# Two edits of an already tuned two-block kernel: first weight halves rounded and split ahead of the mixed groups in the front, and output-projection parts spread over twelve steps of the neighbourhood attention, ahead of each value product

## The chip, the cores and the metric

The kernel runs on one core of one Trainium2 chip. The metric is device time in microseconds (us). All data are 32-bit floats. Engines in the profile: PE is the matrix engine, PEld its weight loads, DVE the vector engine, ACT the scalar engine, POOL the general engine, SP the engine that issues most DMAs.

## The reference

One call runs a block of two layers and then a second block, each on 256 tokens of width 1024. The first layer mixes with a Fourier transform, and this is the front of the kernel:

```python
def mix(h):                       # h = modulate(rms_norm(x), shift, scale)
    hg = h.reshape(b, l, FNET_GROUPS, FNET_GROUP_DIM)          # 8 groups of 128
    y = jnp.fft.fftn(hg, axes=(1, 3), norm='ortho').real
    return y.reshape(b, l, D_MODEL) @ w_out + b_out
x = x + g1 * mix(h);  x = x + g2 * swiglu(...)                 # the context tokens likewise
...                                                            # second layer: differential attention, swiglu
```

Shift, scale and gates are columns of `silu(c) @ w_ada + b_ada`. The second block projects its input once, runs a latent attention (`y_mla`, 8 heads) and a neighbourhood attention (`y_na`, 16 heads), and ends with

```python
h_res = h_res + jnp.concatenate([y_mla, y_na], axis=-1) @ w_out[l]
```

Of this last product the latent half (`y_mla`) can be formed before the neighbourhood attention is done.

## The kernel before

**How a weight gets to PE.** Each float product is made of three products of shorter floats: with `wh` the rounded weight and `wl` the rest, and `hh`, `hl` the same of the activation, `product` (L496 to L500) issues `wh*hh`, `wh*hl` and `wl*hh` into one PSUM bank. SP loads weights in slabs of 1 MB into four slots of `raw`; a slab has two halves. `round_half` (L476) lets ACT write a half into `wh`, and `split_low` (L483) lets DVE write `wl = raw - wh`. There are four slots of `wh` and `wl`, so halves 0 to 3 can stand ready at once.

**What sets the order.** Every engine runs a list written out by hand, strictly in the order of the code; engines meet at semaphores (`split` counts halves split, `s_f2v` groups split, `s_part` parts added, and so on). There is no scheduler: a moved line of code is a moved instruction on that engine, and what stands behind a waiting instruction waits too.

**The front.** x and the context are turned by PE; ACT and DVE make sums and differences of token halves; `fnet_inner(g)` (L2291) transforms group g over tokens into bank 4 or 5, and ACT (even g, L1723) or DVE (odd g, `inner_out`, L1977) copies it into `ab`. DVE scales two groups at a time by gain and shift (`inner_scaled`, L1985 to L1989). `fnet_outer(g)` (L2305, L2307) transforms over the 128 channels into bank 4 + g % 2. Then per group: ACT copies the sines and the edge columns (L1733, L1734; `s_f2q`), DVE writes `mixed` from cosines and sines (L2002, L2003; `s_f2d`), ACT rounds `mixed` to `hh` (L1739; `s_f2a`), DVE subtracts to `hl` (L2006; `s_f2v`). The last four DVE steps of a group stand in one function, `outer_split`. `fnet_dense(k)` multiplies group k by the first four halves of `fnet_w_out`: for m = 0 to 3 three products into bank m; with k = 0 each m first waits for `split` to reach m + 1. PE's list there: outer(0), outer(1), ada_slab(4), ada_slab(5), dense(0), ada_slab(6), ada_slab(7), outer(2), ada_turn(1), dense(1), outer(3), dense(2), and on to dense(7).

**The modulation weights in the front.** `ada_slab(i)` (L2245) multiplies a 1 MB slab of `w_ada`, 24 of them in the front; they pass through slots of `raw`, `big` and `ex`, and SP issues a load (L1502) only when the slab before it in its slot has been used. Weight slabs of `fnet_w_out` (L489) share SP's list: slabs 0 and 1 after ada slabs 0 and 1 are used, slabs 2 and 3 after ada slabs 6 and 7 are used.

**The neighbourhood attention.** `na_pe`, `na_act` and `na_dve` run steps i = 0 to 19; 16 of them have scores. In step i PE forms the scores of step i (L1325), turns the weights of step i - 2 (L1337, L1340; "the turn"), in even steps multiplies by the values (L1351, L1356; "the value product") and then runs `latent_part(g, k)` (L1296 to L1298) as often as `PART_AT[i]` says. A part is three products of 512 columns into bank 7; four parts (k = 0 to 3) make a quarter g of the latent output, and DVE adds it to `x_tok` (`latent_added`, L1311). Part (g, 0) waits for the quarter before it to be added (`s_part`). The value product waits for ACT's copies of the turned weights (L1384, L1386), ACT's copy in an even step waits for the value product of that step, and parts of g = 3 free the first halves of the output weights, whose successors ACT rounds in steps 13 to 16 (`ROUND_AT`).

Of the kernel before, what the change touches and what calls it, by code (L numbers as in the profile page):

```python
# [185 lines left out]
def build(nc, d, out):  # L186

    with ExitStack() as ctx:
# [1088 lines left out]
        PART_AT, parts = {}, [(g, k) for g in range(4) for k in range(4)]  # L1277
        for i in range(4, 15):
            n = 1 + i % 2
            PART_AT[i], parts = parts[:n], parts[n:]  # L1280
# [32 lines left out]
        def na_pe(pe, tail):  # L1313

            pe.wait_ge(s_gap, 1)
            for i in range(NA_STEPS + 4):
# [11 lines left out]
                if 2 <= i < NA_STEPS + 2:  # L1328
# [10 lines left out]
                    for c in range(2):  # L1339
                        ins = nc.tensor.transpose(ps[0:n, 4 + j0 % 2, (2 + c) * P:(3 + c) * P],  # L1340
                                                  ex3[:, j0 % 3, c, side:side + n], T["ident"])
                    ins.then_inc(s_tr, 1)
                if i % 2 == 0 and 0 <= (i - 4) // 2 < 8:
                    f = (i - 4) // 2
# [13 lines left out]
                    ins.then_inc(s_pv, 1)  # L1358
                for g, k in PART_AT.get(i, ()):
                    latent_part(pe, g, k)  # L1360
                tail(i)
# [321 lines left out]
        def _(act):  # L1683
# [37 lines left out]
            for g in range(0, KD, 2):  # L1721
                act.wait_ge(s_f1, g + 1)
                nc.scalar.activation(ab[:, g, :, :].rearrange("p s n -> p (s n)"), ps[:, 4, :], ACT.Copy)\  # L1723
                    .then_inc(s_f1a, 1)
            for q in range(2):
                round_half(act, q, q)
            for g in range(KD):
                act.wait_ge(s_f2, g + 1)
                if g >= 2:
                    act.wait_ge(s_f2v, g - 1)  # L1730
                m = mixed[:, g % 2, :].rearrange("p (s n) -> p s n", s=2)
                b = 4 + g % 2
                nc.scalar.activation(sines(g), ps[:, b, 2 * P + 2:4 * P], ACT.Copy)  # L1733
                nc.scalar.activation(m[:, :, 0:P + 1:P],  # L1734
                                     ps[:, b, 0:2 * P + 2].rearrange("p (s n) -> p s n", s=2)[:, :, 0:P + 1:P],
                                     ACT.Copy).then_inc(s_f2q, 1)
                act.wait_ge(s_f2q, g + 1)
                act.wait_ge(s_f2d, g + 1)
                nc.scalar.activation(by_column(hh[:, g, 0:NT]), by_row(mixed[:, g % 2, :]), ACT.Copy).then_inc(s_f2a, 1)  # L1739
                if g < AHEAD - 2:  # L1740
                    round_half(act, g + 2, g + 2)
            for m, q in enumerate(FNET_OUT_Q):
# [125 lines left out]
        def _(dve):  # L1868
# [30 lines left out]
            def ada_copy(gi):  # L1899

                dve.wait_ge(s_adau, ADA_GROUPS[gi]["end"])
                positive(dve, s_adat, gi)
                nc.vector.tensor_copy(ada_row, ps[:, 6, :]).then_inc(s_adac, 1)
# [87 lines left out]

            def outer_split(g):

# [8 lines left out]
                nc.vector.tensor_tensor(m[:, :, 1:P], cos[:, :, 1:P], sin, ALU.subtract)  # L2002
                nc.vector.tensor_tensor(m[:, :, L - 1:P:-1], cos[:, :, 1:P], sin, ALU.add).then_inc(s_f2d, 1)  # L2003
                dve.wait_ge(s_f2a, g + 1)
                dve.wait_ge(s_f2d, g + 1)
# [16 lines left out]
            inner_out(7)  # L2022
            inner_scaled(2)
            split_low(dve, 0, 0)
            outer_split(0)
            split_low(dve, 1, 1)
            outer_split(1)
            split_low(dve, 2, 2)
            split_low(dve, 3, 3)
            ada_copy(1)  # L2030
            outer_split(2)
            ada_group_out(1)
            dve.wait_ge(s_adav, 4)
            scaled_gain(0, 0, 4, 4)
            inner_scaled(4)
            outer_split(3)
            inner_scaled(6)
            for g in range(4, KD):
                outer_split(g)
            ada_copy(2)  # L2040
# [183 lines left out]
        def _(pe):  # L2224
# [71 lines left out]
            def fnet_outer(g):  # L2296
# [3 lines left out]
                if g < 2:  # L2300
                    pe.wait_ge(s_f1v if g else s_f1a, 4)
                else:
                    pe.wait_ge(s_f2v, g - 1)
                o = ps[:, 4 + g % 2, :]
# [332 lines left out]
```

## Time and profile before

| | |
|---|---|
| median of 3 runs | 1225.83 us (1225.41 to 1228.3) |
| the profiled execution, whole | 1225.37 us |
| its span, first to last instruction | 1223.7 us |
| PE busy | 1163.9 us, 95% |
| DVE, ACT, POOL busy | 716.5, 547.3, 92.9 us |
| share of PE in the chain that ended last | 82% |
| HBM | 180.48 MB read, 148 GB/s over the span |

All clock readings in the text are microseconds from the span's start in this one execution. The profiled execution lies 0.46 us under the median.

### The profile page before, as it was taken

Reading aid. Unit: us, or ns where it says so; the run is one execution under the profiler, and the core shown is the slowest. Engines: PE = TensorE matmul, PEld = TensorE weight load, DVE = VectorE, ACT = ScalarE, POOL = GpSimd, SP = SyncE. Lnnn points to the kernel's source line nnn. Section 1 sums busy time; section 2 is a strip of 40 time slices with the busy share of each in tenths; the row PEclk is TensorE's granted clock in tenths of the full one; section 3 lists DMA queues with packets and bytes.
Section 4 is the critical chain, followed back from the end, with each engine's and each line's share of the span. In section 5 each row is a group of like instructions: output and inputs, shape, how many; then the busy total and the mean of one; then the engine's idle time right before and its main releaser. Section 6 shows DMA issues by size and latency. Waiting matters only on the chain.

```text
span 1223.7 us, 18598 instructions
## 1 busy us (share of the span) xinstructions
PE 1163.9 (95%) x7032; PEld 968.7 (79%) x7032; DVE 716.5 (59%) x1207; ACT 547.3 (45%) x1022; POOL 92.9 (8%) x137
## 2 busy tenths in 40 slices
PE   7899999999999999799998889999988999999998
PEld 4565787787788888578985789999988986799766
DVE  6664577767723334767669664455567475445673
ACT  4353422222222323554448654444456576466662
POOL 0002011122100000200000010000010000120410
PEclk9999999999999999899999999999999999999999
DMA  8899355678623322133330156555444443164220
GB/s 310 317 328 324 136 159 188 190 250 282 240 71 103 103 87 85 35 104 103 104 104 1 46 166 200 173 189 173 162 138 130 151 125 103 44 202 148 97 70 34
DMA packets 121669, 182.81 MB, mean 149 GB/s; under 512 B 4497, under 2 KB 92896, under 8 KB 121600
## 3 DMA queue, kind: packets, MB, share of 16 engines
q1 hardware_dynamic: 113888, 154.44, 38.2%
q0 software_dynamic: 7712, 27.43, 6.8%
q8 instruction: 45, 0.74, 0.3%
q14 instruction: 24, 0.20, 0.1%
HBM read 180.48 MB, written 1.05 MB: 148 GB/s over the span
## 4 chain that ended last, share of the span: by engine, by line
PE 82%; DVE 8%; ACT 5%; issue 3%; POOL 1%; DMA 1%; DVEq 0%; SPq 0%; ACTq 0%; POOLq 0%
PE ps L498 20%; PE ps L499 20%; PE ps L500 20%; PE ps L828 2%; PE ps L829 2%; PE ps L830 2%; PE ps L869 2%; PE ps L2245 1%; ACT wh L476 1%; DVE wl L483 1%; PE ps L2578 1%; PE ps L2580 1%; DVE nrm L612 1%; PE ps L2579 1%; DVE nm L1141 1%
## 5 line engine op out<-in xcount | busy, mean ns | idle before, releaser
L498 PE MATMUL ps<-hh,wh 128*128 128x256 f32 (+2 forms) x1272 | 425.3, 334 | 20.6 <-DVE hl L628 9.6
L483 DVE TENSOR_TENSOR wl<-raw,wh 128x1024 fp32r<-128x1024 f32 (+1 forms) x246 | 295.8, 1207 | 250.9 <-ACT wh L476 247.8
L499 PE MATMUL ps<-hl,wh 128*128 128x256 f32 (+2 forms) x1272 | 416.1, 327 | 0.0
L500 PE MATMUL ps<-hh,wl 128*128 128x256 f32 (+2 forms) x1272 | 415.0, 326 | 0.0
L476 ACT ACTIVATE wh<-raw 128x1024 fp32r<-128x1024 f32 (+1 forms) x246 | 252.5, 1031 | 272.9 <-PE ps L500 261.4
L498 PEld LDWEIGHTS ps<-hh,wh 128*128 128x128 f32 x1272 | 241.1, 190 | 63.1 <-issue 23.5
L500 PEld LDWEIGHTS ps<-hh,wl 128*128 128x128 f32 x1272 | 241.6, 190 | 21.2
L499 PEld LDWEIGHTS ps<-hl,wh 128*128 128x128 f32 x1272 | 240.4, 189 | 22.5 <-issue 1.9
L498 PE MATMUL ps<-ah,wh 128*128 128x256 f32 (+2 forms) x376 | 125.9, 335 | 1.1 <-DVE big L2065 0.8
L499 PE MATMUL ps<-al,wh 128*128 128x256 f32 (+2 forms) x376 | 124.3, 330 | 0.0
L500 PE MATMUL ps<-ah,wl 128*128 128x256 f32 (+2 forms) x376 | 124.2, 330 | 0.0
L498 PEld LDWEIGHTS ps<-ah,wh 128*128 128x128 f32 x376 | 70.6, 188 | 9.2 <-DVE big L2065 1.0
L500 PEld LDWEIGHTS ps<-ah,wl 128*128 128x128 f32 x376 | 70.6, 188 | 7.3
L499 PEld LDWEIGHTS ps<-al,wh 128*128 128x128 f32 x376 | 70.8, 188 | 7.1
L2071 DVE TENSOR_TENSOR al<-big,ah 128x512 fp32r<-128x512 f32 (+1 forms) x42 | 23.3, 558 | 81.3 <-ACT ah L1766 81.3
L1766 ACT ACTIVATE ah<-big 128x512 fp32r (+3 forms) x42 | 21.8, 524 | 103.4 <-PE ps L500 103.4
L828 PE MATMUL ps<-wh,hh 128*128 128x256 f32 (+1 forms) x224 | 65.9, 294 | 1.9 <-DVE nrm L927 1.8
L829 PE MATMUL ps<-wl,hh 128*128 128x256 f32 (+1 forms) x224 | 62.7, 280 | 0.0
L830 PE MATMUL ps<-wh,hl 128*128 128x256 f32 (+1 forms) x224 | 62.7, 280 | 0.0
L650 POOL TENSOR_TENSOR big<-sq 128x512 f32<-128x512 f32 (+2 forms) x4 | 4.8, 1198 | 647.6 <-ACT sq L567 647.6
L927 DVE SCALAR_TENSOR_TENSOR big<-ps,par,rstd 128x256 f32<-128x256 f32 (+3 forms) x60 | 22.6, 405 | 42.7 <-ACT rstd L907 42.7
L828 PEld LDWEIGHTS ps<-wh,hh 128*128 128x128 f32 (+1 forms) x224 | 39.1, 175 | 4.9 <-DVE nrm L927 2.4
(253 smaller groups left out, 1419.8 us busy)
## 6 DMA issues: line engine op xcount, KB each, us to landing
raw<-in_ffn_w_in SPq DMA_DIRECT2D x44, 1024.0 KB, 5.2
raw<-in_ffn_w_out SPq DMA_DIRECT2D x22, 1024.0 KB, 4.9
raw<-in_w_in SPq DMA_DIRECT2D x22, 1024.0 KB, 5.4
big<-in_w_ada SPq DMA_DIRECT2D x16, 1024.0 KB, 11.0
big<-in_w_ada POOLq DMA_DIRECT2D x24, 512.0 KB, 4.4
ex<-in_w_ada POOLq DMA_DIRECT2D x24, 512.0 KB, 5.0
raw<-in_diff_w_in SPq DMA_DIRECT2D x12, 1024.0 KB, 5.1
raw<-in_w_out SPq DMA_DIRECT2D x8, 1024.0 KB, 4.8
```

The source lines that it names most:

```text
L476: ins = nc.scalar.activation(place(wh), v, ACT.Copy)
L483: ins = nc.vector.tensor_tensor(place(wl), v, place(wh).bitcast(F32), ALU.subtract)
L498: nc.tensor.matmul(o, w_hi, m_hi, start=first, stop=False, **kw)
L499: nc.tensor.matmul(o, w_hi, m_lo, start=False, stop=False, **kw)
L500: return nc.tensor.matmul(o, w_lo, m_hi, start=False, stop=last, **kw)
L828: nc.tensor.matmul(oo, mh[:, k, tok], cols(wh), start=first, stop=False)
L829: nc.tensor.matmul(oo, mh[:, k, tok], cols(wl), start=False, stop=False)
L830: ins = nc.tensor.matmul(oo, ml[:, k, tok], cols(wh), start=False, stop=last)
L869: nc.tensor.matmul(ps[0:m, 3 + h % 2, 0:u["w"]], T[u["red"]][0:m, 0:m], sq[0:m, h % 2, 0:u["w"]], start=True, stop=True).then_inc(s_usum, 1)
L927: ins = nc.vector.scalar_tensor_tensor(out=dst, in0=o[:, a:b], scalar=par_of(u["gain"])[0:m, :], in1=rstd[0:m, u["h"] % 2, a:b], op0=ALU.m ...
L1766: nc.scalar.activation(ah[:, at % 2, 0:n], big[:, bass.ds(k * n, n)], ACT.Copy)\
L2071: nc.vector.tensor_tensor(al[:, at % 2, 0:n], big[:, bass.ds(k * n, n)], ah[:, at % 2, 0:n].bitcast(F32), ALU.subtract).then_inc(s_as, 1)
```

## The change

In the front:
- ACT rounds halves 0 and 1 between its copies of inner groups 4 and 6, half 2 after the copy of group 6, and half 3 behind the sines of group 0. Before, halves 0 and 1 came after the last copy, half 2 after `hh` of group 0 and half 3 after `hh` of group 1.
- DVE's `outer_split` becomes `outer_mirrored` (the two steps that write `mixed`) and `outer_low` (the subtraction). For groups 0 and 1 they are placed among the four `split_low`, and `inner_scaled(2)` moves from ahead of all of them to behind them.
- PE's `fnet_outer(g)` for g of 2 and more waits for `mixed` of group g - 2 (`s_f2d`) and no longer for its `hl` (`s_f2v`).

In the neighbourhood attention:
- the 16 parts stand in steps 4 to 15 (before 4 to 14), at most two in a step; part (2, 0) is in step 10, not with (1, 3) in step 9, and each part from there on is one place later;
- within a step the parts come after the turn and ahead of the value product.

```diff
-        for i in range(4, 15):
-            n = 1 + i % 2
+        for i, n in zip(range(4, 16), (1, 2, 1, 2, 1, 1, 1, 2, 1, 2, 1, 1)):
             PART_AT[i], parts = parts[:n], parts[n:]
...
                     ins.then_inc(s_tr, 1)
+                for g, k in PART_AT.get(i, ()):
+                    latent_part(pe, g, k)
                 if i % 2 == 0 and 0 <= (i - 4) // 2 < 8:
...
                     ins.then_inc(s_pv, 1)
-                for g, k in PART_AT.get(i, ()):
-                    latent_part(pe, g, k)
                 tail(i)
...
-            for q in range(2):
-                round_half(act, q, q)
+                if g == 4:
+                    round_half(act, 0, 0)
+                    round_half(act, 1, 1)
+            round_half(act, 2, 2)
             for g in range(KD):
...
+                if g == 0:
+                    round_half(act, 3, 3)
                 act.wait_ge(s_f2q, g + 1)
...
-                if g < AHEAD - 2:
-                    round_half(act, g + 2, g + 2)
...
-            inner_scaled(2)
             split_low(dve, 0, 0)
-            outer_split(0)
+            outer_mirrored(0)
             split_low(dve, 1, 1)
-            outer_split(1)
+            outer_low(0)
+            outer_mirrored(1)
             split_low(dve, 2, 2)
             split_low(dve, 3, 3)
+            outer_low(1)
+            inner_scaled(2)
             ada_copy(1)
...
                 else:
-                    pe.wait_ge(s_f2v, g - 1)
+                    pe.wait_ge(s_f2d, g - 1)
```

Line numbers of the changed kernel differ by 1 to 9 from those of before. ACT in the front, before; `wh<-raw` rounds a half, `big<-ps` copies inner groups, `hh<-nrm` rounds a mixed group:

```order
L1723 ACTIVATE big<-ps 128x512 [waits fnet_inner] x4
L476 ACTIVATE wh<-raw 128x1024 [waits slab_landed_0] x2
L1733 ACTIVATE sq<-ps 128x254 [waits fnet_outer]
L1734 ACTIVATE nrm<-ps 128x4
L1739 ACTIVATE hh<-nrm 128x2x4x64 [waits fnet_mixed,fnet_sines_out]
L476 ACTIVATE wh<-raw 128x1024 [waits slab_landed_1]
```

and ACT at the same place in the changed kernel:

```order
L1722 ACTIVATE big<-ps 128x512 [waits fnet_inner] x3
L476 ACTIVATE wh<-raw 128x1024 [waits slab_landed_0] x2
L1722 ACTIVATE big<-ps 128x512 [waits fnet_inner]
L476 ACTIVATE wh<-raw 128x1024 [waits slab_landed_1]
L1734 ACTIVATE sq<-ps 128x254 [waits fnet_outer]
L1735 ACTIVATE nrm<-ps 128x4
L476 ACTIVATE wh<-raw 128x1024 [waits slab_landed_1]
L1742 ACTIVATE hh<-nrm 128x2x4x64 [waits fnet_mixed,fnet_sines_out]
```

All four roundings now stand ahead of the first `hh`. DVE from the last inner copy on, before; `wl<-raw,wh` splits a half:

```order
L1977 COPY big<-ps 128x512 [waits fnet_inner]
L1985 TENSOR_SCALAR big<-big,gsc 128x256 [waits fnet_inner_out_dve,fnet_inner_out_act]
L1985 TENSOR_SCALAR big<-big,gsc 128x256 x3
L1989 SCALAR_TENSOR_TENSOR big<-ada,big 128x4 [waits dve_chain]
L483 TENSOR_TENSOR wl<-raw,wh 128x1024 [waits half_rounded]
L2002 TENSOR_TENSOR nrm<-ps,sq 128x2x127 [waits fnet_sines_out,fnet_outer]
L2003 TENSOR_TENSOR nrm<-ps,sq 128x2x127
L2006 TENSOR_TENSOR hl<-nrm,hh 128x2x4x64 [waits fnet_mixed,fnet_rounded]
```

and DVE from the same copy on in the changed kernel:

```order
L1978 COPY big<-ps 128x512 [waits fnet_inner]
L483 TENSOR_TENSOR wl<-raw,wh 128x1024 [waits half_rounded]
L2003 TENSOR_TENSOR nrm<-ps,sq 128x2x127 [waits fnet_sines_out,fnet_outer]
L2004 TENSOR_TENSOR nrm<-ps,sq 128x2x127
L483 TENSOR_TENSOR wl<-raw,wh 128x1024 [waits half_rounded]
L2010 TENSOR_TENSOR hl<-nrm,hh 128x2x4x64 [waits fnet_mixed,fnet_rounded]
L2003 TENSOR_TENSOR nrm<-ps,sq 128x2x127 [waits fnet_sines_out,fnet_outer]
L2004 TENSOR_TENSOR nrm<-ps,sq 128x2x127
L483 TENSOR_TENSOR wl<-raw,wh 128x1024 [waits half_rounded] x2
L2010 TENSOR_TENSOR hl<-nrm,hh 128x2x4x64 [waits fnet_mixed,fnet_rounded]
L1986 TENSOR_SCALAR big<-big,gsc 128x256 [waits fnet_inner_out_dve,fnet_inner_out_act]
```

The scaling of groups 2 and 3 has gone behind the splits, and between `mixed` and `hl` of a group stands other work. PE in step 9 of the neighbourhood attention and the start of step 10, before, from part (1, 3) on:

```order
L1296 MATMUL ps<-wh,hh 128x512
L1297 MATMUL ps<-wl,hh 128x512
L1298 MATMUL ps<-wh,hl 128x512
L1296 MATMUL ps<-wh,hh 128x512 [waits latent_part_added]
L1297 MATMUL ps<-wl,hh 128x512
L1298 MATMUL ps<-wh,hl 128x512
L1325 MATMUL ps<-big 128x176 [waits row_max]
L1325 MATMUL ps<-big 128x176
L1337 MATMUL ps<-tab,ex 128x128 [waits weights_copied,weights_ready]
L1337 MATMUL ps<-tab,ex 128x128
L1340 MATMUL ps<-tab,ex 48x128 x2
L1351 MATMUL ps<-x_ctx,tab 64x256 [waits o_scaled,side_values_landed,weights_copied]
```

and PE from the same part on in the changed kernel:

```order
L1295 MATMUL ps<-wh,hh 128x512
L1296 MATMUL ps<-wl,hh 128x512
L1297 MATMUL ps<-wh,hl 128x512
L1324 MATMUL ps<-big 128x176 [waits row_max]
L1324 MATMUL ps<-big 128x176
L1336 MATMUL ps<-tab,ex 128x128 [waits weights_copied,weights_ready]
L1336 MATMUL ps<-tab,ex 128x128
L1339 MATMUL ps<-tab,ex 48x128 x2
L1295 MATMUL ps<-wh,hh 128x512 [waits latent_part_added]
L1296 MATMUL ps<-wl,hh 128x512
L1297 MATMUL ps<-wh,hl 128x512
L1352 MATMUL ps<-x_ctx,tab 64x256 [waits o_scaled,side_values_landed,weights_copied]
```

Part (2, 0), the one with the wait, has moved behind the scores and the turn of step 10 and stands ahead of its value product.

## Rows read from the trace of the kernel before

**Rows 1.** The page: busy time of the engines over the span.
```profile
PE 1163.9 (95%) x7032; PEld 968.7 (79%) x7032; DVE 716.5 (59%) x1207; ACT 547.3 (45%) x1022; POOL 92.9 (8%) x137
```

**Rows 2.** Timeline of PE, front: start, length, instructions, [idle before <- releaser].
```profile
36.67 1.06 PE L2245 MATMUL ps<-ex,big 128*32 128x512 f32 x8 [0.36 <-DMA ex<-in_w_ada]
39.38 0.50 PE L498 MATMUL ps<-hh,wh 128*128 128x512 f32 x1 [1.65 <-DVE hl L2006]
...
40.51 0.50 PE L498 MATMUL ps<-hh,wh 128*128 128x512 f32 x1 [0.17 <-DVE wl L483]
...
44.62 0.50 PE L498 MATMUL ps<-hh,wh 128*128 128x512 f32 x1 [3.15 <-DVE wl L483]
...
47.34 2.47 PE L2245 MATMUL ps<-raw,big 128*32 128x512 f32 x16
...
51.54 0.48 PE L498 MATMUL ps<-hh,wh 128*128 128x512 f32 x1
...
90.33 2.78 PE L2245 MATMUL ps<-big 128*32 128x512 f32 x24
```

**Rows 3.** Busy time by stretch: PE busy, granted clock, DMA share, GB/s.
```profile
46.00:47.00 1.00, 1.00 (x3) 0.50 0.05 20
```

**Rows 4.** Timeline of ACT in the front, columns as in Rows 2.
```profile
32.15 0.60 ACT L1723 ACTIVATE big<-ps 128x512 f32<-128x512 f32 x1 [3.27 <-PE ps L2291]
...
34.80 0.18 ACT L1734 ACTIVATE nrm<-ps 128x4 f32<-128x4 f32 x1
37.05 1.14 ACT L1739 ACTIVATE hh<-nrm 128x512 fp32r<-128x512 f32 x1 [2.08 <-DVE nrm L2003]
37.97 1.07 ACT L476 ACTIVATE wh<-raw 128x1024 fp32r<-128x1024 f32 x1
```

**Rows 5.** Timeline of DVE in the front.
```profile
33.76 1.13 DVE L1985 TENSOR_SCALAR big<-big,gsc 128x256 f32<-128x256 f32 x4
...
35.08 1.22 DVE L483 TENSOR_TENSOR wl<-raw,wh 128x1024 fp32r<-128x1024 f32 x1
...
38.22 1.10 DVE L2006 TENSOR_TENSOR hl<-nrm,hh 128x512 fp32r<-128x512 f32 x1 [1.26 <-ACT hh L1739]
...
43.36 2.35 DVE L483 TENSOR_TENSOR wl<-raw,wh 128x1024 fp32r<-128x1024 f32 x2
```

**Rows 6.** Three loads by line and stretch: issue, then time to landing.
```profile
L489 SPq DMA_DIRECT2D raw<-in_fnet_w_out x1: 368/368/368, 21.9 to 21.9; - x1
DMA to landing us min/median/max: 5.3/5.3/5.3
...
L1502 SPq DMA_DIRECT2D raw<-in_w_ada x1: 726/726/726, 29.3 to 29.3; - x1
DMA to landing us min/median/max: 12.7/12.7/12.7
...
L1502 SPq DMA_DIRECT2D big<-in_w_ada x1: 368/368/368, 82.9 to 82.9; - x1
DMA to landing us min/median/max: 7.5/7.5/7.5
```

**Rows 7.** Busy time by stretch: PE, PEld, DVE, ACT, POOL, clock, DMA share, GB/s.
```profile
1145.00:1155.00 10.00, 8.60 (x63) 5.62 (x64) 8.28 (x27) 8.14 (x27) 7.08 (x14) 1.00 0.32 107
```

**Rows 8.** Timeline of PE in the neighbourhood attention, steps 4, 5, 9 and 16, columns as in Rows 2.
```profile
1148.10 0.65 PE L1351 MATMUL ps<-x_ctx,tab 112*64 112x256 f32 x4 [1.36 <-ACT x_ctx L1386]
...
1149.12 0.50 PE L1296 MATMUL ps<-wh,hh 128*128 128x512 f32 x1
...
1150.01 0.60 PE L1325 MATMUL ps<-big 64*128 64x192 f32 x4
...
1164.28 0.50 PE L1296 MATMUL ps<-wh,hh 128*128 128x512 f32 x1 [1.38 <-DVE x_lat L1311]
...
1181.23 0.44 PE L1337 MATMUL ps<-tab,ex 128*128 128x128 f32 x2 [0.86 <-DVE ex L1419]
```

**Rows 9.** Timeline of DVE there, step 10.
```profile
1163.55 0.68 DVE L1311 TENSOR_TENSOR x_lat<-ps,x_lat 128x512 f32<-128x512 f32 x1
```

More of the change, by code:

```diff
@@ L1990, in inner_scaled, with outer_mirrored @@
                                                in1=first, op0=ALU.mult, op1=ALU.add).then_inc(s_f1s, 2)
-            def outer_split(g):
+            def outer_mirrored(g):
                 b = 4 + g % 2
@@ L2003, in outer_split, with outer_low @@
                 nc.vector.tensor_tensor(m[:, :, L - 1:P:-1], cos[:, :, 1:P], sin, ALU.add).then_inc(s_f2d, 1)
+            def outer_low(g):
                 dve.wait_ge(s_f2a, g + 1)
@@ L2022, in _ @@
             inner_out(7)
-            inner_scaled(2)
             split_low(dve, 0, 0)
-            outer_split(0)
+            outer_mirrored(0)
             split_low(dve, 1, 1)
-            outer_split(1)
+            outer_low(0)
+            outer_mirrored(1)
             split_low(dve, 2, 2)
             split_low(dve, 3, 3)
+            outer_low(1)
+            inner_scaled(2)
             ada_copy(1)
-            outer_split(2)
+            outer_mirrored(2)
+            outer_low(2)
             ada_group_out(1)
@@ L2035, in _ @@
             inner_scaled(4)
-            outer_split(3)
+            outer_mirrored(3)
+            outer_low(3)
             inner_scaled(6)
             for g in range(4, KD):
-                outer_split(g)
+                outer_mirrored(g)
+                outer_low(g)
             ada_copy(2)
```

## The prediction

> **What bounds the kernel now.** The page is read first: PE is busy 95% of the span [rows 1], so the change can only win what PE does not use, 60 us in all, at the places it touches. There are two, and for each the timeline of PE is read, then those of the engines it waited for.
>
> In the front PE ends the modulation slabs ahead of `fnet_dense(0)` at 36.67 + 1.06 = 37.73 and starts `fnet_dense(1)` at 51.54 [rows 2]: 13.81 us. In it stand three idle pieces: 1.65 until `hl` of group 0 is there, 0.17 for half 1, 3.15 for half 2 [rows 2]. Behind the long one the granted clock reads 0.50, the 1.2 GHz level, where it read 1.00 (2.4 GHz) before [rows 3]; of the two slabs at 47.34 part is still slow.
>
> In the neighbourhood attention PE waits 1.36 in step 4 for ACT's copy of turned weights, 1.38 in step 9 because part (2, 0) wants bank 7 back, and 0.86 in step 16 for DVE [rows 8]. In between it runs without a gap.
>
> **The front, step by step.** No instruction is added or removed.
>
> *ACT.* It is free from 28.88 (idle 3.27 ahead of the copy at 32.15 [rows 4]). Halves 0 and 1 need slab 0, landed at 21.9 + 5.3 = 27.2 [rows 6]. Two roundings of some 1 us (a row has 1.07 with its tail [rows 4]) end near 30.9, ahead of the copy at 32.15, which is not delayed. Half 2 fills 32.7 to 33.7, where ACT worked on halves 0 and 1 before. The sines of group 0 end at 34.98 as now [rows 4]. Half 3 follows until 35.9.
>
> *DVE.* At 33.76 it now splits half 0 (1.22 with its tail, 1.13 from start to start) in place of the scaling of groups 2 and 3, which took 1.32 until the split at 35.08 [rows 5]. It waits for the sines until 35.03, writes `mixed` of group 0 until 35.8 (now it does so behind the split at 35.08, which costs 1.2 more), and splits half 1 until 36.9.
>
> *ACT again.* `hh` of group 0 starts at 35.9 instead of 37.05 and takes 1.14 [rows 4]: done at 37.0. `hl` starts at 37.05 instead of 38.22 and takes 1.10 [rows 5]: done at 38.15. **dense(0) starts at 38.2, not 39.38**; its first two groups need halves 0 and 1, there since 36.9. A group of three products takes 1.13 - 0.17 = 0.96 [rows 2], two in a row some 1.55.
>
> *DVE again.* `hl` holds it until 38.05, `mixed` of group 1 until 38.7; then halves 2 and 3, two in 2.35 [rows 5], are done at 39.95 and 41.1. PE takes group m = 2 at 40.0 (now 44.62) and m = 3 at 41.1, and is through at 41.95. What is left of idle time is 0.5 + 0.3 + 0.2 = 1.0.
>
> *Slabs 6 and 7, outer(2), ada_turn(1).* From 47.34 to 51.54 they take 4.20 [rows 2], part of it at the low clock. At the high clock a slab takes 0.93 (2.78 for three at 90.33 [rows 2]), so two take 0.6 less than the 2.47 there with the tail: about 3.8. The later of the slabs landed at 29.3 + 12.7 = 42.0 [rows 6] and is used at 42.9. The scaling that was moved back ends at 43.4, ahead of outer(2) at 43.9, so what was moved is covered, by half a microsecond. dense(1) starts at 41.95 + 3.8 = 45.75, with `hl` of group 1 done at 42.1. **Gain of the front: 51.54 - 45.75 = 5.8 us.** I take 5.7.
>
> PE's new wait of outer(g) is the weaker one and costs nothing: from 51.54 on PE was not held by `hl`. Every load behind this place is issued when PE has used a slot, so SP's list moves with PE: the two weight slabs that follow slabs 6 and 7 are issued near 43 and not at 49.
>
> Bounds: 6.7 if dense(0) runs whole from 38.2 (2.9 us); 4.0 if the clock still falls. Its price is 1.7: the two groups from 44.62 to 47.34 took 2.72 [rows 2] where two in a row take some 1.55 to 1.6, and the slabs behind lost 0.6.
>
> **The neighbourhood attention.** Step 4: part (0, 0) moves into the 1.36 of waiting. Its cost from its start to the next scores is 1150.01 - 1149.12 = 0.89 [rows 8]; the value product cannot start before 1148.10, and its end meets the wait for the scores instead. **Gain 0.8.** Bounds 0.6 and 0.9.
>
> Step 9: part (2, 0) waits for `latent_added(1)`, which DVE runs at 1163.55 for 0.68 [rows 9], behind its own work of step 9. In the changed kernel PE does the scores and the turn of step 10 meanwhile, about 1.05 of work, before it asks; some 0.3 to 0.6 of waiting stay. **Gain 1.0.** Bounds 0.7 and 1.4.
>
> Steps 13 to 17: every part behind (2, 0) comes one place later, so part (3, 3) falls into step 15, ahead of the idle 0.86 [rows 8]. That hole takes its 0.7. But in an even step ACT's copy waits for a value product that is now a part later, and ACT's roundings of steps 14 and 15 with it; DVE has the last `latent_added` in front of the last weights, behind a split. By the same chaining the last turn comes 0.4 later than PE could otherwise have it. **Gain 0.3.** Bounds -0.5 and 0.7.
>
> The other even steps: the same work with the same number of waits in another order, 0.0 to 0.1 each for four steps, taken as 0.2. Bounds -0.3 and 0.6. Sum of the attention: 0.8 + 1.0 + 0.3 + 0.2 = **2.3 us**, bounds 0.5 and 3.6.
>
> **Sum.** 5.7 + 2.3 = 8.0. The profiled execution took 1225.37, 1.67 outside its span; 1225.37 - 8.0 = 1217.4. The median of the runs lies 0.46 above the profiled one, so its like would be 1217.8; I say 1217.6.
>
> **Rivals.**
>
> *The clock falls all the same.* dense(0) still has three gaps. They are 0.5 at most where the fall came behind 3.15, and in 1145 to 1155, with 1.4 of 10 us idle, the clock reads 1.00 [rows 7]. 1217.6 + 1.7 = 1219.3.
>
> *The transfers don't follow.* Slab 17 is issued at 82.9, lands 7.5 later at 90.4 [rows 6], and is wanted as the third of three at 90.33 + 1.86 = 92.2 [rows 2]: 1.8 us to spare. If its landing is set by the queue and not by PE's freeing of the slot, the front keeps 1.8 of 5.7: 1221.5. Against it: the issue follows the use of slab 12 in the same buffer, so it comes earlier with PE.
>
> *The attention gives nothing.* ACT (8.14 of 10) and DVE (8.28) are loaded in its densest stretch, where PE is at 8.60 [rows 7]; with ACT's copy behind a later value product, ACT could become the pace and six parts of 0.7 come back as waiting. The gain of 2.3 is then gone, and up to 1 more: 1219.9 to 1220.9. Against: that stretch holds two roundings which the other steps lack, and 1.9 of its 10 us are still free on ACT.
>
> The Trainium skill, page "TensorE: Matmul & The Clock Gate" (Architectural detail: the array is 16× 32×32, not 1× 128×128), calls the queues of ScalarE and VectorE strictly first in, first out, where PE may pull weight loads ahead. By that rule alone, ready exponentials stand behind ACT's waiting copy in every even step, and the attention would come out at this rival's 1220.9; by the free 1.9 us of the row it comes out at the sum's 2.3. The trace shows the rule at work in the front, where ACT idles 3.27 ahead of a copy though roundings stand ready behind it [rows 4].
>
> *Slower than before.* ACT works in order, and halves 0 and 1 now stand ahead of the copy of inner group 6, which outer(0) and all behind it need. The margin is 32.15 - 30.9 = 1.25 us: with slab 0 landing later than about 30.1 instead of 27.2 [rows 6], each microsecond is one of PE. It becomes slower than before from a landing past 38. With a landing at 42.0, when the last load of that batch lands [rows 6], ACT is 11.8 late: 1217.6 + 11.8 = 1229.4. Slab 0 is the first load in the queue there, which speaks against it.
>
> *The change doesn't do what it says:* something not seen holds PE at 47, and only the attention moves: 1223.
>
> **How the numbers follow.** Forecast 0.66; clock 0.10; transfers 0.05; attention nothing 0.10; more than forecast, with the upper bounds of both parts (1215) 0.05; not as said 0.03; slower 0.01. The forecast's own range is 1216.2 to 1219. For 8 in 10 it reaches to the clock and attention cases: 1215.3 to 1220.8. A measurement of this kernel can tell about 0.3% (3.7 us) from no change: faster means under 1222.1. Faster 0.95, same 0.04, slower 0.01.
>
> **What would show it.** In the trace after: PE starts dense(0) near 38.2, has m = 2 at 40.0 and m = 3 at 41.1, dense(1) near 45.8, and no granted clock of 0.50 between 40 and 50. In the attention the value product of step 4 starts with a part ahead of it, the wait for DVE's addition is under 0.7 in step 10, and the part in step 15 stands in front of the turn of step 16. It is wrong if PE waits for a slab between 42 and 110, if the copy of inner group 6 moves from 32.15, or if idle time in front of the value products grows by more than 0.3 each.

## The result and the profile after

| | before | after |
|---|---|---|
| median of the runs, us | 1225.41 (1224.15 to 1228.3, 5 runs) | 1217.14 (1214.27 to 1219.25, 5 runs) |
| ratio to before, 95% interval | | 0.9929 (0.9911 to 0.9947) |
| profiled execution, us | 1225.37 | 1216.36 |
| its span, us | 1223.7 | 1214.7 |

By the ratio the change makes the kernel 8.7 us faster (6.5 to 10.9). The forecast was 1217.6, with a range of 1215.3 to 1220.8, and the time of the forecast's own case came out.

The page after: the work is the same, the span shorter [rows 1].

```profile
PE 1160.6 (96%) x7032; PEld 967.8 (80%) x7032; DVE 716.4 (59%) x1207; ACT 546.7 (45%) x1022; POOL 92.8 (8%) x137
```

**The front.** Timeline of PE after (start, length, instructions, idle before and its releaser), to be held against [rows 2]:

```profile
37.91 1.07 PE L2254 MATMUL ps<-ex,big 128*32 128x512 f32 x8 [0.56 <-DMA ex<-in_w_ada]
39.28 0.50 PE L498 MATMUL ps<-hh,wh 128*128 128x512 f32 x1 [0.30 <-DVE hl L2010]
...
41.06 0.50 PE L498 MATMUL ps<-hh,wh 128*128 128x512 f32 x1
...
42.20 0.50 PE L498 MATMUL ps<-hh,wh 128*128 128x512 f32 x1 [0.17 <-DVE wl L483]
...
43.10 1.92 PE L2254 MATMUL ps<-raw,big 128*32 128x512 f32 x16
...
46.75 0.48 PE L498 MATMUL ps<-hh,wh 128*128 128x512 f32 x1
```

This execution was 1.25 us late ahead of all this: its slab 5 ends at 37.91 + 1.07 = 38.98, against 37.73 before. From there to dense(1) it is 46.75 - 38.98 = 7.77 us where it was 13.81. The idle pieces of 1.65, 0.17 and 3.15 ahead of the groups m = 0, 1 and 2 are now 0.30, none and none; one of 0.17 ahead of m = 3 is new. The two slabs take 1.92 instead of 2.47, at a clock that holds. Busy time by stretch after (length, PE busy with its instructions, granted clock, DMA share, GB/s), the second row that of [rows 3]:

```profile
40.00:50.00 10.00, 9.70 (x53) 1.00 1.07 372
...
46.00:47.00 1.00, 1.00 (x10) 1.00 1.07 363
```

In 46 to 47 stood 3 instructions at 0.50, the 1.2 GHz level; now 10 at 1.00. What ACT and DVE do there after, as [rows 4] and [rows 5]:

```profile
29.82 1.99 ACT L476 ACTIVATE wh<-raw 128x1024 fp32r<-128x1024 f32 x2
...
33.19 0.60 ACT L1722 ACTIVATE big<-ps 128x512 f32<-128x512 f32 x1 [1.39 <-PE ps L2300]
...
36.92 1.15 ACT L1742 ACTIVATE hh<-nrm 128x512 fp32r<-128x512 f32 x1
```

```profile
38.10 1.12 DVE L2010 TENSOR_TENSOR hl<-nrm,hh 128x512 fp32r<-128x512 f32 x1
...
39.80 2.34 DVE L483 TENSOR_TENSOR wl<-raw,wh 128x1024 fp32r<-128x1024 f32 x2
...
43.07 1.12 DVE L1986 TENSOR_SCALAR big<-big,gsc 128x256 f32<-128x256 f32 x4
```

Halves 0 and 1 are rounded in what was idle time, and 1.39 of it is left ahead of the copy of inner group 6 at 33.19. That copy stands at 32.15 + 1.04: it moved with the late start of this execution, not with the roundings.

**The attention.** Timeline of PE after, steps 4, 6, 10 and 14 to 17 (before: [rows 8]):

```profile
1139.07 0.48 PE L1295 MATMUL ps<-wh,hh 128*128 128x512 f32 x1
...
1140.68 0.65 PE L1352 MATMUL ps<-x_ctx,tab 112*64 112x256 f32 x4 [0.66 <-ACT x_ctx L1385]
...
1144.19 0.57 PE L1324 MATMUL ps<-big 64*128 64x176 f32 x4
...
1146.99 0.59 PE L1324 MATMUL ps<-big 64*128 64x192 f32 x4
...
1155.58 0.50 PE L1295 MATMUL ps<-wh,hh 128*128 128x512 f32 x1 [0.31 <-DVE x_lat L1310]
...
1169.03 0.48 PE L1295 MATMUL ps<-wh,hh 128*128 128x512 f32 x1
...
1171.89 0.65 PE L1352 MATMUL ps<-x_ctx 112*64 112x256 f32 x4 [1.16 <-ACT x_ctx L1385]
...
1173.14 0.60 PE L1336 MATMUL ps<-tab,ex 128*128 128x128 f32 x2 [0.15 <-DVE ex L1418]
...
1173.82 0.77 PE L2587 MATMUL ps<-wh,hh 128*128 128x512 f32 x1
...
1178.09 0.65 PE L1352 MATMUL ps<-x_ctx 112*64 112x256 f32 x4
```

From the scores of step 4 to the first product of the output (L2587) it is 35.76 us, before 38.65. The wait of step 4 fell from 1.36 to 0.66 behind part (0, 0), and that of part (2, 0) from 1.38 to 0.31. At the value product of step 16 the wait for ACT's copy grew from 0.21 to 1.16. ACT's timeline after shows what stands ahead of that copy:

```profile
1168.27 0.38 ACT L1383 ACTIVATE x_ctx<-ps 128x256 f32<-128x256 f32 x1 [0.89 <-PE ps L1357]
...
1169.39 1.04 ACT L476 ACTIVATE wh<-raw 128x1024 fp32r<-128x1024 f32 x1
...
1171.48 0.36 ACT L1385 ACTIVATE x_ctx<-ps 64x256 f32<-64x256 f32 x1
```

A rounding of 1.04 (step 14's, of the output's weights) runs at 1169.39, then exponentials, and only then the copy that PE waits for. In this execution the clock then fell too (columns as above):

```profile
1174.00:1176.00 2.00, 2.00 (x6) 0.50 1.01 416
```

**The whole span** of the profiled pair, 9.0 us: the late start -1.25, the front +6.04, the stretch from dense(1) to the scores of step 4, whose code is untouched but for PE's weaker wait, +2.62 (1093.93 to 1091.31), the attention +2.89, the tail from the first output product on -1.30 (39.58 to 40.88). Only the front and the attention are plainly the change. Whether the 2.62 belongs to it is asked in after_again and in the last section.

### The profile page after: what moved, and what is told of

The parts are those of the page before. It is cut to its first block, busy times and chain, and to the rows that moved or that the text cites. A ratio compares the mean times of both kernels' runs of the same rounds, so it can differ in the third digit from the quotient of the medians.

```text
span 1214.7 us, 18598 instructions
## 1 busy us (share of the span) xinstructions
PE 1160.6 (96%) x7032; PEld 967.8 (80%) x7032; DVE 716.4 (59%) x1207; ACT 546.7 (45%) x1022; POOL 92.8 (8%) x137
## 3 DMA queue, kind: packets, MB, share of 16 engines
HBM read 180.48 MB, written 1.05 MB: 149 GB/s over the span
## 4 chain that ended last, share of the span: by engine, by line
PE 81%; DVE 9%; ACT 5%; issue 3%; POOL 1%; DMA 1%; DVEq 0%; SPq 0%; ACTq 0%; POOLq 0%
PE ps L498 20%; PE ps L500 20%; PE ps L499 20%; PE ps L828 2%; PE ps L829 2%; PE ps L830 2%; PE ps L869 2%; PE ps L2254 1%; ACT wh L476 1%; DVE hl L628 1%; DVE nrm L612 1%; PE ps L2587 1%; PE ps L2589 1%; PE ps L2588 1%; DVE nm L1141 1%
```

## The experiments

Each kernel was timed beside runs of the kernel before. Three numbers are read from each profiled execution: **front**, from the end of slab 5 to dense(1); **attention**, from the scores of step 4 to the first output product; **middle**, the stretch between dense(1) and those scores, untouched but for PE's weaker wait.

| kernel | front | attention | middle | median, us | ratio to before (95%) |
|---|---|---|---|---|---|
| before | 13.81 | 38.65 | 1093.93 | | |
| after | 7.77 | 35.76 | 1091.31 | 1217.14 | 0.9929 (0.9911 to 0.9947) |
| after_again | 7.90 | 35.52 | 1094.23 | 1217.43 | 0.9920 (0.9904 to 0.9935) |
| front_only | 7.89 | 38.64 | 1092.04 | 1219.19 | 0.9940 (0.9926 to 0.9954) |
| attention_only | 13.43 | 35.51 | 1094.20 | 1223.37 | 0.9969 (0.9957 to 0.9982) |
| fill_gap | 12.79 | 38.64 | 1092.05 | 1225.22 | 0.9993 (0.9981 to 1.0005) |
| front_dve | 9.11 | 38.65 | 1092.03 | 1220.01 | 0.9954 (0.9938 to 0.9970) |
| front_act | 14.25 | 38.66 | 1095.63 | 1225.84 | 0.9996 (0.9984 to 1.0008) |
| places_only | 13.64 | 36.81 | 1093.85 | 1224.0 | 0.9981 (0.9971 to 0.9990) |
| ahead_only | 13.90 | 37.65 | 1093.96 | 1225.77 | 0.9998 (0.9980 to 1.0016) |
| old_wait | 7.91 | 35.49 | 1092.15 | 1215.31 | 0.9916 (0.9897 to 0.9935) |
| late_round | 7.99 | 34.39 | 1093.15 | 1214.82 | 0.9897 (0.9882 to 0.9912) |
| late_both | 7.96 | 34.47 | 1093.82 | 1214.39 | 0.9902 (0.9887 to 0.9918) |
| late_first | 7.86 | 34.20 | 1093.79 | 1215.22 | 0.9908 (0.9892 to 0.9925) |

The theory: two local gains, one in the front (most of it waiting, the rest clock) and one in the attention, that simply add. The rivals: the front's gain is mostly the clock's, or comes from one engine's order alone; the attention's comes from the places of the parts alone; and part of the whole is an untouched stretch that happened to be short.

### Each half of the change alone: front_only, attention_only

front_only has the front's edits and the old attention; attention_only is the reverse.

> The front of the change alone; the neighbourhood attention is as before. Theory (the two parts add up): PE starts dense(1) 5.8 to 6.1 us earlier counted from the end of slab 5, no granted clock of 0.50 near 45, and the time is 5.7 us under before, near 1219.7. Rival (much of the gain is luck of the granted clock near 500 and 720, where no code was changed): the front's own move shows in the trace, but the time lies anywhere from 1217 to 1222 with the number of low-clock stretches there, and its runs spread by 3 us or more.

> The attention's part of the change alone; the front is as before. Theory: from the scores of step 4 to the first output half PE needs 35.8 us and not 38.65, of which 1.3 are given back if the granted clock falls at the end of it, as it did in the changed kernel behind a wait of 1.16; time 1.6 to 2.9 under before, 1222.5 to 1223.8. Rival (the attention is paced by ACT and DVE): under 1 us.

The front alone takes 7.89, with the attention at 38.64 as before; the attention alone takes 35.51, with the front at 13.43. Neither touches the other: 5.92 + 3.14 = 9.1 by these readings, and 0.9940 x 0.9969 = 0.9909 by the timed ratios, which multiplied bound by bound reach from 0.988 to 0.9936 and so hold after's 0.9929. In attention_only the low clock begins at 42, before the long gap and not behind it, so PE is slower into the gap ahead of m = 2, and that is 2.71 and not 3.15:

```profile
40.57 0.50 PE L498 MATMUL ps<-hh,wh 128*128 128x512 f32 x1 [1.63 <-DVE hl L2005]
...
41.69 0.57 PE L498 MATMUL ps<-hh,wh 128*128 128x512 f32 x1 [0.16 <-DVE wl L483]
...
45.82 0.79 PE L498 MATMUL ps<-hh,wh 128*128 128x512 f32 x1 [2.71 <-DVE wl L483]
```

### What the clock costs in the front: fill_gap

The kernel before, with products that nobody reads put into the long gap of dense(0), so that PE is busy nearly until half 2 is there. Nothing of the computation is left out.

```diff
+                    if k == 0 and m == 2:
+                        for _ in range(22):
+                            nc.tensor.matmul(ps[:, 7, 256:512], tile_of(wh, 0, KD, P)[:, 0, :], hh[:, 0, 0:256],
+                                             start=True, stop=True)
```

> The kernel before with 22 extra matrix products of 256 columns, whose result nobody reads, in PE's idle piece ahead of group m = 2 of dense(0); nothing else is moved. Theory: the idle piece itself stays closed to useful work, but the granted clock stays at 1.00 from 45 to 48, and dense(1) starts 1.6 to 1.8 us earlier; 1223.7. Rival (the fall has another cause than the idle PE): the clock falls all the same, 1225.4.

Timeline of PE in fill_gap:

```profile
42.02 2.79 PE L2316 MATMUL ps<-hh,wh 128*128 128x256 f32 x22
45.41 0.50 PE L498 MATMUL ps<-hh,wh 128*128 128x512 f32 x1 [0.60 <-DVE wl L483]
...
47.44 1.92 PE L2245 MATMUL ps<-raw,big 128*32 128x512 f32 x16
...
51.09 0.48 PE L498 MATMUL ps<-hh,wh 128*128 128x512 f32 x1
```

With the gap of 3.15 cut to 0.60 the clock does not fall in 45 to 48: the slabs take 1.92. From m = 2 to dense(1) it is 51.09 - 45.41 = 5.68, before 51.54 - 44.62 = 6.92 [rows 2]. So **the low clock costs 1.24 us there**, not the 1.7 of the prediction and the 1.6 to 1.8 of this expectation. Over the whole front 13.81 - 12.79 = 1.0 is left of it, since this execution waited 1.79 for `hl` where before had 1.65, and took 0.08 more from m = 0 to m = 2. The timed ratio can't tell it from nothing.

One pair of executions is not much, but the other traces bear it out. The low clock stands in the front of all five executions that keep DVE's old order and its gap, and there m = 2 to dense(1) takes 6.55 to 7.29: 0.9 to 1.6 above the 5.68. It stands in none of the nine others, fill_gap among them. That the long gap itself makes it fall is not shown by this: in attention_only it fell ahead of the gap. The waits are the greater part of the front's gain: idle pieces of 4.97 before and of 0.41 + 0.18 in front_only make 4.4 of its 5.9, the clock some 1.2, and 0.3 is not assigned.

### Which engine's order carries the front: front_dve, front_act

front_dve has DVE's new order and PE's new wait, and ACT as before; front_act has the early roundings of ACT alone, and this is its edit.

```diff
-            for q in range(2):
-                round_half(act, q, q)
+                if g == 4:
+                    round_half(act, 0, 0)
+                    round_half(act, 1, 1)
+            round_half(act, 2, 2)
...
+                if g == 0:
+                    round_half(act, 3, 3)
...
-                if g < AHEAD - 2:
-                    round_half(act, g + 2, g + 2)
```

> The kernel before with DVE's new order in the front and PE's new wait, but ACT's roundings where they were (halves 0 and 1 behind the last inner copy, half 2 behind hh of group 0, half 3 behind hh of group 1). Theory (most of the gain hangs on DVE's order, since the scaling and the serial pairs stood ahead of the splits): group m = 2 of dense(0) starts within 0.6 of the changed kernel, m = 3 waits 1.4 to 1.7 longer for ACT's rounding of half 3; from the end of slab 5 to dense(1) 9.2 to 9.8 us (before 13.8, changed 7.8). Rival (ACT's early rounding is what frees the front): 12 or more.

> The kernel before with ACT's new order of roundings in the front alone; DVE and PE as before. Theory: DVE still scales groups 2 and 3 first and runs mixed, hl and split in series, so from the end of slab 5 to dense(1) 13.2 to 13.8 us, as before; with the clock 1.0 to 1.7 less or more. Rival (ACT carries the gain): 10 or less.

Timeline of PE in front_dve, then in front_act:

```profile
38.87 0.50 PE L498 MATMUL ps<-hh,wh 128*128 128x512 f32 x1 [0.40 <-DVE hl L2009]
...
40.83 0.50 PE L498 MATMUL ps<-hh,wh 128*128 128x512 f32 x1 [0.30 <-DVE wl L483]
...
43.04 0.50 PE L498 MATMUL ps<-hh,wh 128*128 128x512 f32 x1 [1.25 <-DVE wl L483]
```

```profile
40.44 0.50 PE L498 MATMUL ps<-hh,wh 128*128 128x512 f32 x1 [1.73 <-DVE hl L2008]
...
45.66 0.50 PE L498 MATMUL ps<-hh,wh 128*128 128x512 f32 x1 [3.13 <-DVE wl L483]
...
48.16 3.04 PE L2247 MATMUL ps<-raw,big 128*32 128x512 f32 x16
```

DVE's order alone brings 13.81 - 9.11 = 4.7, the clock's part among it, since the granted clock reads 1.00 from 40 to 50 there. ACT's early roundings alone bring nothing: both old waits stand, 1.73 and 3.13, since DVE still splits late; the 14.25 is 0.44 above before, because the low clock lies over the slabs (3.04 where before had 2.47). On top of DVE's order they are worth 9.11 - 7.8 = 1.3, the 1.25 that m = 3 waits for half 3. The halves of the edit are not a sum: the second pays only behind the first. Both readings lie just outside what was expected (9.11 for 9.2 to 9.8, 14.25 for 13.2 to 13.8) and far from the rivals' 12 or more and 10 or less.

### PE's weaker wait: old_wait

```diff
-                    pe.wait_ge(s_f2d, g - 1)
+                    pe.wait_ge(s_f2v, g - 1)
```

> The changed kernel with PE's wait of fnet_outer(g) put back to hl of group g - 2. Theory: PE never stands at that wait, 7.7 to 8.1 us from slab 5 to dense(1) and the same time as the changed kernel within 0.2 us by the trace. Rival (the weaker wait carries a part): PE idle ahead of outer(2) or outer(3), 8.5 or more.

Front 7.91 against 7.77 and 7.90: the wait is worth nothing, as the prediction had it.

### The two edits of the attention: places_only, ahead_only

places_only gives the parts their new steps, by the edit below; ahead_only puts them ahead of the value product in the old steps.

```diff
-        for i in range(4, 15):
-            n = 1 + i % 2
+        for i, n in zip(range(4, 16), (1, 2, 1, 2, 1, 1, 1, 2, 1, 2, 1, 1)):
```

> The kernel before with the sixteen parts at their new steps (4 to 15), but still behind the value product of a step. Theory: the wait of 1.38 in step 9 goes (under 0.4 left), the wait of 1.36 in step 4 stays, and ACT's copy isn't held, so no wait above 0.4 ahead of the value product of step 16; from the scores of step 4 to the first output half 36.8 to 37.4 us (before 38.65, changed 35.76). Rival (the places don't matter, the order within a step does): 38.3 or more.

> The kernel before with the parts ahead of the value product of a step, at their old steps (4 to 14). Theory: the wait of step 4 shrinks from 1.36 to 0.6 or so, the wait in step 9 stays near 1.4, and ACT's held copy brings a wait of 0.5 to 1.2 ahead of the value product of step 16; 37.2 to 38.2 us from the scores of step 4 to the first output half. Rival (the order within a step carries all): 36.3 or less.

Timeline of PE, the idle pieces of places_only and then of ahead_only:

```profile
1148.20 0.65 PE L1350 MATMUL ps<-x_ctx,tab 112*64 112x256 f32 x4 [1.36 <-ACT x_ctx L1385]
...
1179.84 0.65 PE L1350 MATMUL ps<-x_ctx 112*64 112x256 f32 x4 [0.27 <-ACT x_ctx L1385]
...
1181.98 0.44 PE L1336 MATMUL ps<-tab,ex 128*128 128x128 f32 x2 [1.05 <-DVE ex L1418]
```

```profile
1149.96 0.65 PE L1353 MATMUL ps<-x_ctx,tab 112*64 112x256 f32 x4 [0.65 <-ACT x_ctx L1386]
...
1164.87 0.50 PE L1296 MATMUL ps<-wh,hh 128*128 128x512 f32 x1 [1.39 <-DVE x_lat L1311]
...
1181.25 0.44 PE L1337 MATMUL ps<-tab,ex 128*128 128x128 f32 x2 [0.88 <-DVE ex L1419]
1182.98 0.65 PE L1353 MATMUL ps<-x_ctx 112*64 112x256 f32 x4 [1.07 <-ACT x_ctx L1386]
```

Each edit removes its own wait: the places that of step 9 whole, the order half of that of step 4. The order does one thing more. From the scores of an even step to the next ones, where no wait stands (steps 6, 8, 12 and 14), it is 3.00 or 3.01 us in before and in places_only and 2.79 to 2.82 in after and in ahead_only: 0.2 a step, and it comes with the order alone.

Together 1.84 + 1.00 = 2.84, the change has 2.89 to 3.14. The 1.00 is low because ahead_only had the clock against it too: from the last value product shown to the first output product it took 1184.99 - 1182.98 = 2.01, its instructions long as at the low level, where after_again took 1.65. The last row of ahead_only also tells where after's new wait is from: parts ahead of the value product delay ACT's step 14, and the rounding there delays step 16's copy; with the places alone it is 0.27.

### The new wait at the end: late_round

The output's roundings of steps 14 and 15, and DVE's splits of them, are both done in step 15, whose place is behind the copy.

```diff
-        ROUND_AT = {2: [-2], 3: [-1], 13: [0], 14: [1], 15: [2], 16: [3]}
+        ROUND_AT = {2: [-2], 3: [-1], 13: [0], 15: [1, 2], 16: [3]}
```

> The changed kernel with one more edit: ACT's rounding (and DVE's split) of the second half-weight of the last part goes from step 14 to step 15, behind the copy for the value product of step 16. Theory: the wait of 1.16 ahead of that product is the rounding (1.05) standing in front of the last exponentials and the copy; it falls under 0.3, and with it goes the low clock behind it; 1.2 to 2.3 us under the changed kernel, 1215 to 1216. Rival (the copy was late because of the value product that now comes a part later): the wait stays above 0.8, no gain.

Timeline of ACT, then of PE, in late_round:

```profile
1173.78 0.36 ACT L1385 ACTIVATE x_ctx<-ps 64x256 f32<-64x256 f32 x1
1174.05 2.00 ACT L476 ACTIVATE wh<-raw 128x1024 fp32r<-128x1024 f32 x2
```

```profile
1174.20 0.65 PE L1352 MATMUL ps<-x_ctx 112*64 112x256 f32 x4 [0.22 <-ACT x_ctx L1385]
...
1175.67 0.48 PE L2587 MATMUL ps<-wh,hh 128*128 128x512 f32 x1
...
1178.67 0.65 PE L1352 MATMUL ps<-x_ctx 112*64 112x256 f32 x4
```

The cause is shown: with the rounding behind the copy the wait falls from 1.16 to 0.22 and the attention to 34.39, 1.1 under after_again; the 0.15 for DVE behind it is gone too. The next stretch, from the first output product to the next value product, takes 1178.67 - 1175.67 = 3.00 at the high clock, where the profiled execution of after took 1178.09 - 1173.82 = 4.27. after_again, with the same code as after and the clock high, took 2.97. So the low clock behind the wait cost after 1.3 in this stretch and 0.3 ahead of it (1.93 from the value product to the first output product, against 1.65). This is the fastest of all kernels here by its ratio, 0.9897, and its interval only just meets after's. The three kernels with the late rounding have 0.9897, 0.9902 and 0.9908, the three without it 0.9916, 0.9920 and 0.9929. So the traces show that it is better than the change, and the times make it likely without proving it.

### The wait that is left in step 4: late_both, late_first

PE still waits 0.66 for ACT's copy in step 4. late_both moved the rounding of step 3 back by one step, late_first that of step 2 into step 3; both keep late_round's edit.

```diff
-        ROUND_AT = {2: [-2], 3: [-1], 13: [0], 14: [1], 15: [2], 16: [3]}
+        ROUND_AT = {2: [-2], 4: [-1], 13: [0], 15: [1, 2], 16: [3]}
```

```diff
-        ROUND_AT = {2: [-2], 3: [-1], 13: [0], 14: [1], 15: [2], 16: [3]}
+        ROUND_AT = {3: [-2, -1], 13: [0], 15: [1, 2], 16: [3]}
```

> The changed kernel with two roundings moved: that of step 14 to step 15 (as in the run late_round) and that of step 3 to step 4, behind the copy for the first value product. Theory: the wait of 0.66 ahead of the value product of step 4 is the same case, a rounding in front of exponentials and copy, and falls to 0.2 or less; DVE's split of that half may hold part (0, 3) by 0.2; 33.9 to 34.3 us from the scores of step 4 to the first output half (late_round 34.39, changed 35.76). Rival (the wait is the latency of the first steps): the wait stays, 34.4 or more.

> The kernel of late_round with the rounding of step 2 also moved, to step 3, so that both roundings there come behind ACT's second copy. (late_both had moved the one of step 3, which already stood behind that copy, and left the one of step 2 ahead of it.) Theory: the wait of 0.66 ahead of the value product of step 4 is the rounding of step 2, and is gone; DVE's two splits now stand in step 4 together and may hold the turn of step 5 or the second part of step 5 by 0.3; 33.5 to 34.1 us from the scores of step 4 to the first output half (late_round 34.39). Rival (latency of the first steps): the wait stays, 34.4 or more.

Timeline of PE in late_both, then in late_first:

```profile
1141.79 0.65 PE L1352 MATMUL ps<-x_ctx,tab 112*64 112x256 f32 x4 [0.66 <-ACT x_ctx L1385]
```

```profile
1141.49 0.65 PE L1352 MATMUL ps<-x_ctx,tab 112*64 112x256 f32 x4
...
1146.05 0.44 PE L1336 MATMUL ps<-tab,ex 128*128 128x128 f32 x2 [0.47 <-DVE ex L1418]
```

late_both moved the wrong one, and the wait did not change: step 3's rounding already stands behind the copy. late_first moved the right one, and the wait is gone. But 0.47 comes back two steps later, because DVE now has both splits in a row. Its timeline in late_first:

```profile
1142.20 2.60 DVE L483 TENSOR_TENSOR wl<-raw,wh 128x1024 fp32r<-128x1024 f32 x2 [0.70 <-ACT wh L476]
...
1145.47 0.53 DVE L1418 TENSOR_TENSOR ex<-ex,rc 128x352 f32<-128x352 f32 x1
```

0.2 us stay (34.39 to 34.20), which no timing here can tell.

### The same kernel again: after_again

> The changed kernel once more, unaltered. Theory (the 2.6 us that the first pair of profiles differs between dense(1) and the attention, where no code was changed, is the granted clock falling into other places in each execution): front 7.7 to 8.1 us from slab 5 to dense(1) and 35.4 to 35.8 us in the attention, as in its first profile, but the stretch between is longer or shorter by up to 2 us, with the low clock elsewhere. Rival (the change makes the middle shorter): the stretch again near 1091.3.

Front and attention repeat within 0.25 us. The middle does not: 1094.23, against 1091.31 with the same code. That is 2.9, where the expectation allowed 2. So the profiled pair's 2.62 is not what the change brings each time; how far it was luck, the last section asks. The low clock at 1174 did not come back either.

## Why the prediction was right

**dense(0) at 38.2.** 39.28, less the 1.25 of this execution's late start, is 38.03. The chain came out by its steps: `hh` 36.92, `hl` 38.10 for 1.12, each some 1.05 behind the predicted start. Right.

**m = 2 at 40.0, m = 3 at 41.1, 1.0 idle left.** 41.06 and 42.20, less 1.25: 39.8 and 40.95. The idle pieces left are 0.30 + 0.17 = 0.47 instead of 1.0. Some more is hidden: m = 0 to m = 2 takes 41.06 - 39.28 = 1.78, where the working had 1.55 for two groups in a row.

**dense(1) at 45.75.** 46.75 - 1.25 = 45.5. Gain 6.04 in the pair, 5.92 in front_only, against the working's 5.8, of which 5.7 was taken. The scaling that was moved back runs from 43.07 and PE does not wait for it; the cover of half a microsecond held.

**The clock's price** was the term that was wrong in the front. The 1.7 was 2.72 against some 1.6 for two groups, and 0.6 for the slabs. fill_gap measured 1.24: there the two groups take 47.44 - 45.41 = 2.03 and not 1.6, since the wait ahead of m = 3 stays, which is 0.69; the slabs, 2.47 to 1.92, are 0.55. It did not enter the forecast, only the lower bound (4.0) and the rival. That rival (1219.3) fell: the clock reads 1.00 through 40 to 50 in after. The executions with the low clock in the front span 0.9 to 1.6, so the 1.7 lies above all of them.

**The attention's terms.** They are read from scores to scores, with 0.7 for a part that changed its step. Step 4: 0.8 predicted; from its scores to those of step 5 it is 4.54 before and 3.64 after, so 0.9, the upper bound. The value product stands where the working had it: it comes 2.62 behind the scores of step 4 (1138.06 to 1140.68), before 2.63. Steps 9 and 10: 1.0 predicted with 0.3 to 0.6 of waiting left; 0.31 is left, and 7.17 became 5.19 + 0.7, so 1.3. From the scores of step 15 on: 0.3 predicted. The idle pieces there went from 0.86 + 0.21 + 0.52 = 1.59 to 1.16 + 0.15 = 1.31, but by the marks 4.93 + 0.7 became 5.73 in after, with its low clock, and 5.46 in after_again: -0.1 and 0.2. The size is near and the way is not: the hole of step 16 went wholly, and a wait for ACT took most of it back, by the chaining that the prediction named as the reason for its lower bound. It named the roundings of steps 14 and 15 as work that comes later, and not that one of them would hold the copy. One of its signs of being wrong was met here: idle time in front of this value product grew by 0.95, from 0.21 to 1.16, where it allowed 0.3 each. At the other value products it did not grow.

**The other even steps: mis-sized.** 0.2 was taken for the four of them together. Between the scores of step 6 and those of step 7, without a wait in either kernel, it is 3.00 us before (1152.50 to 1155.50) and 1146.99 - 1144.19 = 2.80 after, and steps 8, 12 and 14 have the same 0.2. That is 0.8 in all, above the term's upper bound of 0.6, and ahead_only has it without the new places. The terms then close: 0.9 + 1.3 + 0.8 and -0.1 or 0.2 are 2.9 and 3.2, where the marks say 2.9 and 3.1. The total, against 2.3 predicted, stayed within its 3.6. In the timelines a value product directly behind the turn starts 0.31 us after the turn's last instruction began, a part 0.14. Why was not tested.

**The rule on queues.** For the attention the prediction weighed the rule of the Trainium skill, page "TensorE: Matmul & The Clock Gate" (Architectural detail: the array is 16× 32×32, not 1× 128×128), that ScalarE's and VectorE's queues are strictly first in, first out. In the steps from 6 to 14 the trace shows no wait at a value product, so ACT's slack covered it there, as the row on its load [rows 7] let one expect. In step 16 the trace shows a wait of 1.16 of just that kind, and moving one rounding behind the copy took 0.94 of it away. The trace agrees with the rule; what it costs hangs on what is queued ahead of the copy.

**The other rivals.** The transfers follow: with the front 6 us earlier PE waits for no slab between 42 and 110, as before, and front_only keeps its whole gain. ACT's order did not become the bound: 1.39 of idle time is left ahead of the copy of inner group 6, with 1.25 predicted.

**The total.** 6.0 + 3.0 = 9.0 of trace against 8.0 predicted. That 1217.6 met 1217.14 so closely owes something to chance: the runs of after alone spread over 5 us, and the even steps gave 0.6 more than was taken for them.

## What to carry to other kernels

Where TensorE waits for operands that two other engines make one after the other, write both lists out and look for work whose consumer comes later than the next wait: moving a scaling and splitting a helper in two was worth 4.7 us here, an earlier start of the first engine alone nothing. In a loop of small unlike groups, try their order too: a ready group between the turn and the value product gave 0.2 us in each even step without any wait being there. Of every long step in an in-order list (a rounding of 1.04 us) ask which short one behind it is waited for; putting it behind that copy was worth 1.1 us. What a low clock around a gap costs is told by filling the gap: 1.24 us here, where the gap itself was 3.15.

## What the runs showed of the hardware

**Untouched code varies by some 4 us between executions, and the granted clock goes with it.** The middle took 1091.31 to 1095.63 with the same instructions. Its clock falls in few places. Busy time by stretch (PE, PEld, DVE, ACT, POOL, clock, DMA share, GB/s) of after:

```profile
480.00:520.00 40.00, 33.59 (x130) 24.66 (x129) 27.83 (x59) 21.32 (x43) 6.42 (x5) 0.96 0.16 53
```

- With 0.91 in that stretch and 1.00 from 900 to 1000 the middle is 1092.0 to 1092.2 (front_only, fill_gap, front_dve, old_wait).
- With 0.91 and 0.98 from 900 to 1000 it is 1093.8 to 1094.2 (after_again, late_both, late_first), and 1093.15 in late_round, which has 1.00 from 700 to 740 where the others have 0.95 or 0.96.
- With 0.87 and 1.00 it is 1093.9 or 1094.0 (before, places_only, ahead_only), with 0.87 and 0.98 it is 1095.63 (front_act).
- after has 0.96 and the shortest, 1091.31. Attention_only has 0.91 and 1.00 and yet 1094.20; its clock reads 0.99 from 600 to 700.

The reading 0.87 comes of one more fall, near 500, and costs 1.9 us; the fall between 900 and 1000 costs 1.7 to 2.2. This makes single traces useless for totals under some 4 us. The distance between two near marks repeats to 0.2 or 0.3 with the same code, and to 0.5 where the clock falls between them (13.43 to 13.90 in the front of before's order).

**How much of the 2.62 was luck stays open.** The 0.87 stands in four of the five executions that had the low clock in the front, and in none of the nine that had not. So 1.9 us of the middle may follow from the front, and only the other 0.7, from the shorter fall that after alone had, would be plain luck. after_again is no proof against it: it has 0.91 too, and took 1094.23 with the fall behind 900. What speaks against it is fill_gap, whose profiled execution had the high clock in the front and a middle of 1092.05. By its marks it should gain 1.0 + 1.9 = 2.9, and by its times it gains at most 2.3 (0.9981). No run tested it.

**Waits of about 1 us in the attention were followed by the low clock in two executions and not in three others.** It came behind 1.16 in after and behind 1.07 (with 0.88 less than 2 us ahead of it) in ahead_only, and not behind 1.17 in after_again and attention_only or 1.16 in old_wait, though all but ahead_only run the same code there. In the front it came behind 1.63 and 0.16 in attention_only, and behind 3.15 and 3.13 in before and front_act. So a short wait late in a kernel can cost its own length again and more (1.6 in after), or nothing.

**What else stays open.** By the times front_only gains 7.3 us (0.9940 of 1227), by its marks 5.9; attention_only 3.8 and 3.1. Both differences are inside the intervals.
